# The first layer's input in a two-layer encoder trunk: norm gain multiplied into the projection's weights, all x tiles loaded at once

## What is computed

```python
def _rmsnorm(x, g):
    y = xf * lax.rsqrt(jnp.mean(xf * xf, axis=-1, keepdims=True) + RMS_EPS)
    return y * g

for i in range(DEPTH):                     # DEPTH = 2
    h = _rmsnorm(x, norm_mix[i])
    # layer 0: qkv = h @ w_in  (1024 x 1536: 16 query heads, 4 key heads, 4 value heads of 64)
    #          rotary positions on q and k, attention in a window, @ w_out
    x = x + mix
    h = _rmsnorm(x, norm_ffn[i])
    x = x + _swiglu(h, ffn_w_gate_up[i], ffn_w_down[i])
```

## Time and profile before

| | |
|---|---|
| median of three runs | 2385.79 us |
| the profiled execution | 2387.84 us |
| its span, first to last instruction | 2385.8 us |
| TensorE matmuls busy | 2276.6 us, 95% |
| VectorE busy | 1286.1 us, 54% |
| ScalarE busy | 894.6 us, 37% |
| GpSimd busy | 564.7 us, 24% |
| mean granted TensorE clock | 0.984 of full speed |

### The profile page before, as it was taken

One profiled execution on the slowest core, in us unless ns is written; L12 is line 12 of the kernel. 1 busy time (PEld: TensorE's weight loads), 2 busy tenths in 40 slices (PEclk: granted clock), 3 DMA queues, 4 the chain that ended last, 5 costly groups with the idle time before them and its releaser, 6 DMA issues.

```text
span 2385.8 us, 33205 instructions
## 1 busy us (share of the span) xinstructions
PE 2276.6 (95%) x11560; PEld 1846.2 (77%) x11560; DVE 1286.1 (54%) x1981; ACT 894.6 (37%) x1622; POOL 564.7 (24%) x420
## 2 busy tenths in 40 slices
PE   4898898999999999999999999999899999999998
PEld 3786676888888788887888777768688888878886
DVE  6566758654444534336332488866854455443422
ACT  3015533433333312232121488854433333331222
POOL 3122332332223000120000266643233233200011
PEclk7999999999999999999999999999899999999999
DMA  5332152222322343233443666654032222252311
GB/s 185 82 92 66 72 150 80 80 79 84 96 84 79 135 169 110 79 98 103 145 143 107 172 158 157 158 173 149 36 106 79 79 79 79 88 201 94 128 48 76
DMA packets 268727, 261.17 MB, mean 109 GB/s; under 512 B 32480, under 2 KB 237536, under 8 KB 263664
## 3 DMA queue, kind: packets, MB, share of 16 engines
q1 hardware_dynamic: 252288, 220.23, 31.2%
q10 hardware_dynamic: 16368, 40.01, 4.5%
HBM read 187.92 MB, written 65.08 MB: 106 GB/s over the span
## 4 chain that ended last, share of the span: by engine, by line
PE 87%; DVE 8%; DMA 2%; ACT 1%; issue 1%; ACTq 1%; POOL 1%; SPq 0%; DVEq 0%
PE psum L1733 12%; PE psum L1735 12%; PE psum L1734 12%; PE psum L2005 11%; PE psum L2007 11%; PE psum L2009 11%; PE psum L1910 3%; PE psum L1884 3%; PE psum L1983 2%; PE psum L1984 2%; PE psum L1985 2%; PE psum L1843 1%; PE psum L1844 1%; DVE b_full L1463 1%; DVE set_lo L1482 1%
## 5 line engine op out<-in xcount | busy, mean ns | idle before, releaser
L2005 PE MATMUL psum<-b_hi,a_hi 128*128 128x512 f32 x1232 | 485.4, 394 | 20.0 <-DVE b_lo L1448 20.0
L2007 PE MATMUL psum<-b_lo,a_hi 128*128 128x512 f32 x1232 | 483.6, 393 | 0.0
L2009 PE MATMUL psum<-b_hi,a_lo 128*128 128x512 f32 x1232 | 483.3, 392 | 0.0
L2005 PEld LDWEIGHTS psum<-b_hi,a_hi 128*128 128x128 f32 x1232 | 233.7, 190 | 72.1 <-issue 23.5
L1733 PE MATMUL psum<-set_hi,dw_hi 128*128 128x512 f32 x704 | 274.7, 390 | 3.5 <-DVE set_lo L1482 3.5
L1735 PE MATMUL psum<-set_hi,dw_lo 128*128 128x512 f32 x704 | 273.9, 389 | 0.0
L1734 PE MATMUL psum<-set_lo,dw_hi 128*128 128x512 f32 x704 | 273.9, 389 | 0.0
L2009 PEld LDWEIGHTS psum<-b_hi,a_lo 128*128 128x128 f32 x1232 | 233.9, 190 | 49.3
L2007 PEld LDWEIGHTS psum<-b_lo,a_hi 128*128 128x128 f32 x1232 | 233.9, 190 | 48.8 <-issue 0.5
L729 POOL TENSOR_TENSOR score<-score,inv_l 128x128 f32<-128x128 f32 (+7 forms) x128 | 152.3, 1205 | 366.6 <-DVE inv_l L1316 366.2
L762 POOL TENSOR_TENSOR a_sum<-a_raw 128x512 f32<-128x512 f32 x88 | 114.9, 1305 | 495.9 <-DVE a_lo L1443 443.4
(11 more groups left out here) (208 smaller groups left out, 3745.4 us busy)
## 6 DMA issues: line engine op xcount, KB each, us to landing
a_raw<-in_ffn_w_gate_up SPq DMA_DIRECT2D x88, 512.0 KB, 5.0
hid_scr<-hid_out SPq DMA_DIRECT2D x44, 512.0 KB, 5.8
set_full<-hid_scr SPq DMA_DIRECT2D x22, 1024.0 KB, 6.5
x_t<-x_scr SPq DMA_DIRECT2D x16, 1024.0 KB, 8.0
dw_raw<-in_ffn_w_down SPq DMA_DIRECT2D x32, 512.0 KB, 3.6
x_scr<-x_t ACTq DMA_DIRECT2D x24, 512.0 KB, 2.6
w_raw<-in_fox_w_in SPq DMA_DIRECT2D x22, 512.0 KB, 3.9
w_raw<-in_swa_w_out SPq DMA_DIRECT2D x16, 512.0 KB, 3.6
```

What stands on the lines that cost most here:

```text
L2005: T.matmul(out_ps, a_hi[i][:, j, :], b_hi[i][:, j, :], start=not more and j == 0, stop=False, skip_group_check=True)
L2007: T.matmul(out_ps, a_hi[i][:, j, :], b_lo[i][:, j, :], start=False, stop=False, skip_group_check=True)
L2009: last = T.matmul(out_ps, a_lo[i][:, j, :], b_hi[i][:, j, :], start=False, stop=j == KH - 1, skip_group_check=True)
```

## The change

The gain leaves the input. GpSimd multiplies it into the raw strips 0 to 11 of `w_in`, each once it is loaded and before it is split; strips of other projections are left alone. The high part of a tile is made straight from PSUM on ScalarE, next to the copy to `x_t`, and the low part straight from PSUM on VectorE. x is loaded into eight buffers with no wait between; the transposes use all eight banks, four tiles in turn. The sum of squares of a token is made from the tile as it was loaded, tokens on partitions, in one fused instruction per tile on VectorE, so it is in the layout of the factors at once: `norm_sums` is left out for layer 0. The conversions of the constants move into VectorE's third chunk, and all small DMAs but the first from ScalarE's queue to SP's, behind the rotary tables.

```diff
@@ SP
             for t in range(TT):
-                if t >= 4:
-                    sp.wait_ge(xin_t, t - 3)
-                sp.dma_start(start_x[t % 4][:, :], x_view[t]).then_inc(xin_loaded[t % 4], 16)
-                if t == 3:
-                    load_w(0, 0, strip(w_in_view["swa"], 0))
-                if t == 7:
-                    load_w(1, 1, strip(w_in_view["swa"], 1))
+                sp.dma_start(start_x[t][:, :], x_view[t]).then_inc(xin_loaded[t], 16)
+                if t in (2, 6):
+                    load_w(t // 4, t // 4, strip(w_in_view["swa"], t // 4))
             sp.dma_start(rope_cos[:, :], rope[0]).then_inc(rope_in, 16)
             sp.dma_start(rope_sin[:, :], rope[1]).then_inc(rope_in, 16)
+            sp.dma_start(causal[:, :], masks[:, P:2 * P]).then_inc(const_in, 16)
...
@@ GpSimd
-            for t in range(TT):
-                pool.wait_ge(start_copy, t + 1)
-                xs = x_t[:, :, t * P:(t + 1) * P]
-                nc.gpsimd.tensor_tensor(start_sq[:, :, t * P:(t + 1) * P], xs, xs, ALU.mult).then_inc(start_square, 1)
+            def scale_weights(c):
+                pool.wait_ge(w_loaded[c % 2], 8 * (c - c % 2) + 16)
+                nc.gpsimd.tensor_tensor(w_raw[c % 2][:, :, :], w_raw[c % 2][:, :, :],
+                                        gains[:, 0, :].unsqueeze(2).to_broadcast([P, KD, P]), ALU.mult).then_inc(w_scaled, 1)
+            pool.wait_ge(gain_in, 16)
+            for c in range(2):
+                scale_weights(c)
             pool.wait_ge(rope_in, 32)
             for c in range(SWA_IN - SWA_V):
+                scale_weights(c + 2)
                 rope_cosine(c)
@@ ScalarE
             def high(c, p):
-                act.wait_ge(w_loaded[p], 8 * (c - p) + 16)
+                if isinstance(c, int) and c < SWA_IN:
+                    act.wait_ge(w_scaled, c + 1)
+                else:
+                    act.wait_ge(w_loaded[p], 8 * (c - p) + 16)
                 wait(act, mm_done, 2 * c - 2)
...
             for t in range(TT):
...
                 act.wait_ge(xin_t, t + 1)
-                nc.scalar.activation(x_t[:, :, t * P:(t + 1) * P], ps, ACT.Copy).then_inc(start_copy, 1)
-                if t > 0:
-                    start_high(t - 1)
-                if t == 6:
+                nc.scalar.activation(h_hi[here], ps, ACT.Copy)
+                nc.scalar.activation(x_t[here], ps, ACT.Copy).then_inc(start_copy, 1)
+                if t == 3:
                     high(0, 0)
-            start_high(TT - 1)
             high(1, 1)
@@ VectorE
-            dve.wait_ge(gain_in, 16)
             for t in range(TT):
                 dve.wait_ge(start_copy, t + 1)
-                wait(dve, h_ready, t - 1)
-                V.tensor_tensor(start_h[t % 2][:, :, :], x_t[:, :, t * P:(t + 1) * P],
-                                gains[:, 0, :].unsqueeze(2).to_broadcast([P, KD, P]), ALU.mult).then_inc(start_gain, 1)
-                if t > 0:
-                    start_low(t - 1)
-                if t == 6:
+                V.tensor_tensor(h_lo[here], start_ps(t), h_hi[here].bitcast(FP32), ALU.subtract).then_inc(h_ready, 1)
+                wait(dve, start_sum, t)
+                V.tensor_tensor_reduce(out=work_c[:, :], in0=start_x[t][:, :], in1=start_x[t][:, :], scale=1.0, scalar=0.0,
+                                       op0=ALU.mult, op1=ALU.add, accum_out=start_ssq[:, t:t + 1]).then_inc(start_sum, 1)
+                if t == 3:
                     low(0, 0)
-            start_low(TT - 1)
             low(1, 1)
-            for t in range(TT):
-                dve.wait_ge(start_square, t + 1)
-                V.tensor_reduce(ssq_start[:, t * P:(t + 1) * P], start_sq[:, :, t * P:(t + 1) * P].rearrange("p k q -> p q k"),
-                                AX.X, ALU.add).then_inc(start_sum, 1)
@@ TensorE
             for t in range(TT):
-                pe.wait_ge(xin_loaded[t % 4], 16 * (t // 4 + 1))
-                if t >= 2:
-                    pe.wait_ge(start_copy, t - 1)
+                pe.wait_ge(xin_loaded[t], 16)
+                if t >= 4:
+                    pe.wait_ge(start_copy, t - 3)
+                    pe.wait_ge(h_ready, t - 3)
...
-            pe.wait_ge(start_copy, TT)
             def start_wait(h, k):
                 if k == 0:
-                    pe.wait_ge(h_ready, 4 * h + 4)
+                    pe.wait_ge(h_ready, TT if h else TT // 2 + 1)
+                    pe.wait_ge(start_copy, TT if h else TT // 2 + 1)
```

More of the change, by code:

```diff
@@ L84, in trunk @@
         rope_in_part = [at(f"rope_in_part{i}", 152 + 12 * i, [P, SEQ]) for i in range(2)]
-        start_sq = at("start_sq", 120, [P, KD, SEQ])
-        start_x = [at(f"start_x{i}", 152 + 4 * i, [P, D]) for i in range(4)]
+        start_x = [at(f"start_x{i}", 120 + 4 * i, [P, D]) for i in range(TT)]
         gate = [at(f"gate{i}", 140 + 4 * i, [FOX_H, SEQ]) for i in range(8)]
@@ L160, in trunk @@
         no_keys = small("no_keys", [P, P])
+        start_ssq = small("start_ssq", [P, TT])
         part_hi = [at(f"part_hi{i}", 120 + 4 * i, [P, SEQ], F32R) for i in range(2)]
@@ L196, in trunk @@
         const_ready = sem("const_ready")
-        xin_loaded = [sem(f"xin_loaded{i}") for i in range(4)]
+        xin_loaded = [sem(f"xin_loaded{i}") for i in range(TT)]
+        w_scaled = sem("w_scaled")
         xin_t = sem("xin_t")
         start_copy = sem("start_copy")
-        start_square = sem("start_square")
-        start_gain = sem("start_gain")
-        start_hi = sem("start_hi")
         start_sum = sem("start_sum")
@@ L287, in trunk, with norm_ssq, start_ps @@
         SQ_USED = (0, 14, 30, 44, 60)
+        def norm_ssq(k):
+            return bank[5] if k else start_ssq
+        def start_ps(t):
+            return psum[:, t % 4 * D:(t % 4 + 1) * D].rearrange("p (k q) -> p k q", q=P)
         def norm_tiles(part):
@@ L843, in norm_root @@
             def norm_root(k, part=None):
-                act.wait_ge(nat_done, NORM_SEQ[k, part] + 1)
+                if k == 0:
+                    act.wait_ge(start_sum, TT)
+                else:
+                    act.wait_ge(nat_done, NORM_SEQ[k, part])
                 c = norm_cols(part)
-                nc.scalar.activation(nat_y[:, c], bank[5][:, c], ACT.Sqrt, bias=eps_c[:, :], scale=1.0 / D)\
+                nc.scalar.activation(nat_y[:, c], norm_ssq(k)[:, c], ACT.Sqrt, bias=eps_c[:, :], scale=1.0 / D)\
                     .then_inc(sd_done, 1)
@@ L1112, in _ @@
             act.dma_start(gains[:, 0:1, :], norm_mix[0:1].rearrange("a (k p) -> p a k", p=P), allow_slow_non_contiguous=True).then_inc(gain_in, 16)
[L1113 to L1126 removed]
             for t in range(TT):
[L1128 removed]
+                ps, here = start_ps(t), (slice(None), slice(None), slice(t * P, (t + 1) * P))
                 act.wait_ge(xin_t, t + 1)
[L1130 to L1133 removed]
+                nc.scalar.activation(h_hi[here], ps, ACT.Copy)
+                nc.scalar.activation(x_t[here], ps, ACT.Copy).then_inc(start_copy, 1)
+                if t == 3:
                     high(0, 0)
[L1135 removed]
             high(1, 1)
@@ L1243, in norm_factor @@
                 dve.wait_ge(sd_done, seq + 1)
-                step(V.tensor_scalar(v, bank[5][:, c], 1.0 / D, EPS, ALU.mult, ALU.add))
+                step(V.tensor_scalar(v, norm_ssq(k)[:, c], 1.0 / D, EPS, ALU.mult, ALU.add))
                 step(V.reciprocal(y, y))
@@ L1741, in norm_sums @@
             def norm_sums(k, part=None):
-                ssq = ssq_start if k == 0 else ssq_ffn if k % 2 else ssq_lin
-                if k == 0:
-                    pe.wait_ge(start_sum, TT)
-                elif part is None:
+                ssq = ssq_ffn if k % 2 else ssq_lin
+                if part is None:
                     pe.wait_ge(sq_used, SQ_USED[k])
@@ L1768, in after0 @@
                 def after0(h):
-                    if norm is not None and h == (1 if norm == 0 else 0):
+                    if norm and h == 0:
                         norm_sums(norm)
```

45 lines of the change are left out of this document (18 added, 27 removed).

## The result

The changed kernel takes 2350.61 us (median of four runs, 2344.5 to 2351.8), the kernel before 2386.91 (median of four, 2383.58 to 2388.73): a ratio of 0.984, interval 0.983 to 0.986. The profiled execution took 2350.45 us with a span of 2347.6. The forecast of 2350.5 is met. It is met less exactly than it looks: the projection gained less than the sum says, and the rest of the program gave some back.

What follows compares the result with a forecast made beforehand. Bound: chunk 2's start on TensorE, held back by ScalarE's queue, VectorE's loop, reductions and column sums. Gains 24.0 + 9.8 + 2.5 = 36.3 us off the median 2385.79 gave 2349.5, plus 1 for unknowns: 2350.5 us, range 2346 to 2359.

Steps and rivals of the forecast that it cites:

- The start of chunk 0: First projection matmul moves from 48.03 to 24.0 us, a gain of 24.0 us.
- The pace: VectorE's low part and fused square per tile in the tile loop: 2 x 1.22 = 2.4 us.
- what GpSimd holds: Two weight scalings during the tile loop delay VectorE by 1.3 us each, between 0 and 2.1.
- the rival of the slow loop: VectorE's tile loop slower than 2.4 us per tile, at 3.0: gain 30.4 us, time 2355.4 us; chance 0.13.
- Chunk 0 to chunk 2: First projection chunks on TensorE: chunk 0 starts at 24.0 us, chunk 2 at 49.8 us.
- The low clock of chunk 0: TensorE starts chunk 0 of the projection at the low clock, costing 2.25 us.
- The hole, the column sums and the second low-clock start: Between chunks 0 and 1 on TensorE: all go, saving 9.8 us for hole and sums, 2.5 for the clock.
- the covers named for tile 7, strip 1 and the factors: Ready before TensorE wants them: tile 7 by 0.4 us, strip 1 at 33.7 against 37.1, factors 37 against 42.6.
- weight strips 2 and 3 become the wait: Constants' DMAs on SP delay strip 2 before chunk 2: 2353 to 2356 us, up to 2362 with strip 3; chance 0.07.
- unknown costs: Allowance of 1 us for GpSimd holding more and first-time waits, added to 2349.5 us.
- The clock being up from the start: All covers hold and TensorE is at full clock from its transposes: gain 39.4, time 2346.4 us; chance 0.08.
- GpSimd as the bound: Scaling and rope product exceed a 10.87 us chunk if scaling is over 8.5 us; slower than before, chance 0.02.

Runs made afterwards that it cites:

- sinks_late: Changed kernel with only the sinks' two DMAs issued later, behind strip 3's load; 2346.57 and 2347.37 us in two runs.
- squares_behind: The kernel with the late sinks, plus VectorE's fused squares moved out of the tile loop, behind low parts of later tiles and of strip 1; 2343.57 us.
- old_squares: Changed kernel with squares as before the change: GpSimd squares, VectorE reduces, TensorE makes the column sums; 2358.99 us.
- consts_on_scalar: Changed kernel with the seven small DMAs back on ScalarE's queue, ahead of its first copy; 2358.51 us.
- strip2_first: Changed kernel with strip 2's load issued on SP ahead of the seven small DMAs; 2347.61 us.

## Why the prediction was right, and where it was not

**The start of chunk 0.** Forecast 24.0 us, measured 22.72. ScalarE's first copy: 7.5 and 7.37 us. The pace: 2.4 us per tile forecast, 2.27 measured; what GpSimd holds: 2.6 us forecast for two scalings, 1.8 us measured (1.25 and 0.56 above 1.21). A PSUM input is not held, as the earlier trace rows had it; the rival of the slow loop fell. The Trainium skill, page "SBUF — State Buffer", section "Who interferes with whom", gives the same division, and here the rows agree on both sides: 2.46 us against 1.21 us.

**Chunk 0 to chunk 2.** 38.0 us before (48.03 to 86.04), 25.8 forecast, 26.25 to the end of chunk 1. The low clock of chunk 0 cost 2.8 us instead of 2.25. The hole, the column sums and the second low-clock start went as the sum had it, and the covers named for tile 7, strip 1 and the factors held: tile 7's low part ended at 29.44 us (forecast 31.3), the diagonal at 34.12 us, wanted at 41.8.

**What failed: the cover of strip 2.** The prediction named who waits for the seven DMAs on SP, the scaling of strip 2, but gave that step no cover in us and no term in the sum; for strips 2 and 3 it took the landing from the earlier trace rows, "those landed in 9.1 us beside other traffic". The landing took 22.9 us. Its own sign of being wrong, that chunk 2 waits for its weight strip, came true. The rival "weight strips 2 and 3 become the wait", with a chance of 0.07, is what happened, though by another way than it was worked out: SP's queue was free again at 22.66 us, earlier than its 24; it was the landing that took longer, for the sinks' two DMAs ahead of the strip and the store beside it. The price was 2.17 us of waiting and then 1.7 us at the lower clock: from the first matmul of chunk 2 to the start of strip 4's high part it took 12.87 us, before the change 97.18 - 86.04 = 11.14. The sum of the projection then reads 25.3 + 11.8 - 2.2 - 1.7 = 33.2 us, and the date in the trace, the same high part, gives 97.18 - 64.01 = 33.2. The forecast was 36.3.

**Why the time is met all the same.** The two profiled executions differ by 37.4 us, so about 4 us come from behind the projection, where the sum had nothing. Lined up by ScalarE's instructions, the two profiles are 33.2 us apart up to 205 us, 34.6 at the start of layer 0's attention, 36.0 at the start of its FFN near 437 us, 34.0 near 1613 us, 38.2 at the end of the spans. The distance changes mostly where the granted clock is below 1.00 (0.98 from 205 to 434 us, 0.94 from 1613 to 1734), and three profiles of the changed kernel with the same first 64 us differ by up to 3.8 us in their spans. The medians hide one thing more: the forecast took 35.3 us (36.3 less 1 for unknown costs) off a median before of 2385.79 us, and 36.3 us came off one of 2386.91. So the hit to 0.1 us is luck; what the trace bears out is 33.2 us in the projection, and what the runs bear out is 36.3 to 37.5 in the medians, with 3 to 4 us that no step of mine explains. What makes the clock fall where it does in the attentions is open; no run was made on it. It may also be why the 4.7 us of sinks_late are only 2.4 to 2.7 in the medians.

**The other rivals.** The clock being up from the start did not happen in the changed kernel (0.50 from 22.7 to 28 us) but did in squares_behind; old_squares, whose first matmul also comes right after the transposes, started at 0.62. GpSimd as the bound did not come near: a scaling takes 1.90 us alone and up to 2.88 in the later chunks, above the 2.4 that the prediction held for the upper end, against a chunk of 10.87.

**What the parts are worth.** From the full change backwards, at the end of chunk 4: the small DMAs' position 11.8 us (consts_on_scalar against sinks_late), the squares 6.4 us, the gain in the weights 3.2 us. They don't add up to 33 and need not: each moves a date that another part would otherwise set. Alone on the kernel before, the small DMAs' position is worth 10 us, and behind it VectorE's loop holds the matmuls for 12.3 us.

## What to carry to other kernels

A DMA that is moved takes more with it than its issue: ask what lands behind it, in its own queue and in the others, and price a small DMA by the landing of one with the same access pattern and not by its bytes: in the changed kernel the sinks' 2 KB took 7.8 and 11.0 us to land, the gains' 4 KB on the same queue 2.5 to 8.3. An idle stretch of the transfers in the profile before, with such a DMA under way, is a warning even where nothing waited for it. Where a wait is the first for TensorE, put ahead of it on each engine only what it needs (here the low parts), and leave the work with a later date (the squares, the sinks) for the time in which TensorE is busy. A wait of 2.2 us in front of TensorE cost 3.9, since the clock fell behind it: count both. And when the total agrees with a forecast, still compare stage by stage; here a gain 3 us too large in the sum and 3 to 4 us from elsewhere cancelled.

## What the runs showed of the hardware

- Two DMAs of single numbers broadcast over 64 partitions each, 4 KB together, kept 4.5 MB of other transfers on two queues standing from about 24 to 31 us, at a busy share of 4.8%. As 64-byte rows the same data, twice over, landed in 3.2 us and held nothing; 4 KB of single numbers without a broadcast landed in 2.5 us, and 4.81 MB passed beside three such DMAs in strip2_first.
- Issuing a 4 KB DMA of single numbers held its queue for between 0.4 and 10.2 us (10.21 us in strip2_first, 4.51 in the earlier trace rows). What sets the length isn't shown: in the changed kernel one at 13.03 us took 0.43 us and the next, at 13.51 us, 3.91, both with the DMA engines busy.
- ScalarE's table load started at 1.27 us where its queue was free, long before the first input was there, and at 19.57 us where DMA issues stood ahead of it.
- Where a GpSimd scaling and VectorE's fused square met, the one that started later paid. At 9.96 us the scaling ran first: it took 1.90 us, as it does alone, and the square from 10.48 us 2.46 instead of 1.21. The scaling at 16.83 us came into a running square (16.29 us, 1.21 us) and took 2.42 us; the square at 18.57 us came into that scaling and took 1.77.
- The fused square and sum of 128x1024 takes 1.21 us plus 0.08 us for reading the sum, so a low part and a square come every 2.27 us.
